# A two-layer hybrid decoder step on one core: output projection joined to the feed-forward network's first half, second half with six and three token tiles per unit of weights, RWKV output beside sample attention

## The reference, cut to what matters

```python
mix = jnp.concatenate([a_out, b_out], axis=-1)      # layer 1: [c_out (RWKV), d_out (sparse attention)]
x = x + mix @ w_out                                 # output projection, 1024 x 1024
...
def conv_ffn(x, g, w_in, conv_w, w_out, buf):       # x = x + conv_ffn(...)
    h = rmsnorm(x, g) @ w_in                        # 1024 -> 2 * 2816
    padded = jnp.concatenate([buf, h], axis=1)
    c = sum(padded[:, i:i + t_len] * conv_w[i] for i in range(3))
    gate, val = jnp.split(c, 2, axis=-1)
    return (jax.nn.silu(gate) * val) @ w_out, padded[:, t_len:]
...
# end of rwkv7_mixer: group norm per head, scale, bonus, gate
y = ((y - mean) * lax.rsqrt(var + RWKV_GN_EPS)).reshape(...) * ln_g + ln_b
out = (y + bonus) * g
```

## Time and profile before

| | us |
|---|---|
| median of 3 runs | 5395.19 (5392.64 to 5398.42) |
| profiled execution | 5434.91 |
| its span, first to last instruction | 5433.3 |
| PE busy | 4338.8 (80%) |
| DVE, ACT, POOL busy | 2336.0 (43%), 1099.4 (20%), 981.7 (18%) |
| mean granted TensorE clock | 0.815 of full speed |

### The profile page before, as it was taken

The page is one execution under the profiler, slowest core; times in us unless marked ns, Lnnn a source line. Parts: engine busy times, 40 slices in busy tenths (PEclk is TensorE's granted clock), DMA queues, the critical chain, the costliest instruction groups (busy, mean ns, idle before and its releaser), DMA issues. The chain is left out here.

```text
span 5433.3 us, 56566 instructions
## 1 busy us (share of the span) xinstructions
PE 4338.8 (80%) x21681; PEld 3367.2 (62%) x21681; DVE 2336.0 (43%) x3548; ACT 1099.4 (20%) x2122; POOL 981.7 (18%) x569
## 2 busy tenths in 40 slices
PE   7799958777899979799748657785276876999799
PEld 6566734335899956577613256775154355999667
DVE  3066431212556521210057567776694134556410
ACT  1132210110111122111034411211253101111221
POOL 2000000000222223222033265000001111222133
PEclk9955556888899989899755567877588987999899
DMA  3211010543111122222233220001313532111120
GB/s 128 79 23 24 12 28 16 161 143 109 48 46 46 35 69 67 85 93 76 83 109 122 99 73 15 28 28 32 109 39 106 159 114 77 46 46 46 61 69 30
DMA packets 239772, 377.90 MB, mean 70 GB/s; under 512 B 107035, under 2 KB 113964, under 8 KB 238191
## 3 DMA queue, kind: packets, MB, share of 16 engines
q1 hardware_dynamic: 213574, 285.77, 17.1%
q0 software_dynamic: 26000, 89.51, 5.3%
HBM read 292.93 MB, written 88.98 MB: 70 GB/s over the span
## 5 line engine op out<-in xcount | busy, mean ns | idle before, releaser
L91 PE MATMUL ffn_up_hp<-ffn_up_xT,ffn_up_w_high 128*128 128x352 f32 x4224 | 1016.1, 324 | 9.5 <-DVE ffn_up_xT L198 9.5
L91 PEld LDWEIGHTS ffn_up_hp<-ffn_up_xT,ffn_up_w_high 128*128 128x128 f32 x4224 | 736.7, 189 | 11.4 <-DVE ffn_up_xT L198 11.4
L91 PE MATMUL ffn_up_hp<-ffn_up_xT,ffn_up_w_low 128*128 128x352 f32 x2112 | 680.2, 322 | 0.0
L91 PEld LDWEIGHTS ffn_up_hp<-ffn_up_xT,ffn_up_w_low 128*128 128x128 f32 x2112 | 399.3, 189 | 0.0
L91 PE MATMUL ffn_down_acc<-ffn_down_w_high,ffn_down_a_high 128*128 128x512 f32 (+1 forms) x792 | 324.1, 409 | 81.4 <-DVE ffn_down_w_low L752 53.3
L91 PE MATMUL od_in_acc<-od_in_w_high,od_in_xT 128*128 128x512 f32 (+3 forms) x1152 | 353.6, 388 | 1.0 <-POOL od_in_w_low L273 1.0
L474 POOL TENSOR_TENSOR ffn_up_w_low<-ffn_up_w,ffn_up_w_high 128x1024 fp32r<-128x1024 f32 x88 | 211.3, 2401 | 756.9 <-DVE ffn_up_w_high L84 756.9
L91 PE MATMUL ffn_down_acc<-ffn_down_w_low,ffn_down_a_high 128*128 128x512 f32 (+1 forms) x792 | 319.4, 403 | 0.0
L91 PE MATMUL ffn_down_acc<-ffn_down_w_high,ffn_down_a_low 128*128 128x512 f32 (+1 forms) x792 | 318.0, 402 | 0.0
L728 POOL TENSOR_TENSOR ffn_down_a_low<-ffn_act_actT,ffn_down_a_high 128x768 fp32r<-128x768 f32 (+2 forms) x144 | 213.2, 1481 | 501.9 <-ACT ffn_down_a_high L700 501.9
L551 ACT ACTIVATE ffn_up_hb<-ffn_up_hp 128x352 f32<-128x352 f32 (+1 forms) x264 | 101.1, 456 | 882.8 <-PE ffn_up_hp L91 882.8
(11 more groups left out here) (573 smaller groups left out, 7993.5 us busy)
## 6 DMA issues: line engine op xcount, KB each, us to landing
ffn_up_w<-ffn_w_in POOLq DMA_DIRECT2D x88, 512.0 KB, 4.8
ffn_down_raw<-ffn_w_out SPq DMA_DIRECT2D x44, 512.0 KB, 3.9
sbs_pages<-cache_sb_k SPq DMA_DIRECT2D x64, 256.0 KB, 2.9
sbs_pages<-cache_sb_v SPq DMA_DIRECT2D x64, 256.0 KB, 3.0
rwkv_arrays<-rwi_out SPq DMA_DIRECT2D x8, 2048.0 KB, 12.3
dsas_pages<-cache_dsa_k SPq DMA_DIRECT2D x64, 256.0 KB, 3.0
dsas_pages<-cache_dsa_v SPq DMA_DIRECT2D x64, 256.0 KB, 3.0
od_in_w<-od_w_in POOLq DMA_DIRECT2D x7, 2048.0 KB, 10.9
```

What stands on the lines that cost most here:

```text
L91: last = nc.tensor.matmul(out, a[p], b[q], start=start and i == 0, stop=stop and i == 2)
```

## The change

Three things change. (1) `project(ev_out)` and `conv_ffn` become one block, `mix_and_ffn`, and od_out likewise: the whole w_mix is loaded in four pieces, all nine tiles are mixed with both column chunks, and each mixed tile is normed and turned from SBUF between the products of the next one. (2) In the second half of the FFN the loops become c, {tiles 0 to 5, tiles 6 to 8}, u, t, with eight accumulators. (3) `rwkv_output` loses its stage; its generators are woven with those of layer 1's sample attention, behind prompt attention. In both sample attentions the query copies take both rounds at once (32 copies for 64), and PE waits for the query and key rows alone.

```diff
-def conv_ffn(nc, name, src, gain, w_in, conv_w, w_out, state, dst, tails, ident_src):
+def mix_and_ffn(nc, name, mix, w_mix, resid, src, gain, w_in, conv_w, w_out, state, dst, tails, ident_src):
...
 @block.gpsimd
 def _(pool):
+    for p in range(PIECES):                                   # PIECES = 4, KP = 2
+        k = slice(p * KP, (p + 1) * KP)
+        pool.dma_start(raw_w[:, k, :], w_mix.rearrange("(k p) n -> p k n", p=P)[:, k, :]).then_inc(o_ld[p], 16)
     for q in range(2):
         load(pool, 0, q)
...
 @block.sync
 def _(sp):
-    s_start(sp)
+    sp.dma_start(ident[:, :], ident_src).then_inc(const_ld, 16)
+    for t in range(2):
+        sp.dma_start(mixed[0:rows_of(t), t, :], mix(t)).then_inc(mix_ld[t], 16)
     sp.dma_start(rows[0:2 * DEC_BATCH, :], state).then_inc(rows_ld, 16)
     sp.dma_start(rows[2 * DEC_BATCH:NR, :], conv_w).then_inc(rows_ld, 16)
-    t_sync(sp)
+    sp.dma_start(gain_b, gain.broadcast_to([P, D_MODEL])).then_inc(const_ld, 16)
+    sp.wait_ge(cols_tr, 1)
+    for t in range(NX1):                                      # NX1 = 3
+        sp.dma_start(x1[0:rows_of(t), t, :], resid(t)).then_inc(res_ld[t], 16)
+    for t in range(TT):
+        if t + 2 < TT:
+            sp.wait_ge(tr_ready, 2 * turn_of["mix", t] + 2)
+            sp.dma_start(mixed[0:rows_of(t + 2), t % 2, :], mix(t + 2)).then_inc(mix_ld[t % 2], 16)
+        sp.wait_ge(x1_ready, 2 * t + 2)
+        sp.dma_start(src(t), x1[0:rows_of(t), t % NX1, :]).then_inc(x1_st[t % NX1], 16)
...
 @block.tensor
 def _(pe):
+    pe.wait_ge(const_ld, 32)
+    turn_tile(pe, "mix", 0)
+    turn_tile(pe, "mix", 1)
     pe.wait_ge(rows_ld, 32)
-    pe.wait_ge(const_ld, 32)
     # 44 transposes of the state and tap rows, wait for DVE's copies of them
+    mixing(pe, 0, range(2))                                   # 48 products
+    for t in range(1, TT):
+        mixing(pe, t, [0])                                    # 24 products
+        if t + 1 < TT:
+            turn_tile(pe, "mix", t + 1)
+        mixing(pe, t, [1])
+        turn_tile(pe, "x1", t - 1)
     up(pe, 0, first=True)                                     # x1 tile 8 is turned before its third block
...
 @block.vector
 def _(dve):
+    turned_parts(dve, "mix", 0)
+    turned_parts(dve, "mix", 1)
     # four copies of the turned state and tap rows
+    for p in range(PIECES):
+        dve.wait_ge(o_high_done, p + 1)                       # ACT makes the high parts
+        nc.vector.tensor_tensor(o_low[:, k, :], raw_w[:, k, :], o_high[:, k, :], ALU.subtract).then_inc(o_low_done, 1)
+    mixed_row(dve, 0)
...
+    for t in range(1, TT):
+        if t + 1 < TT:
+            turned_parts(dve, "mix", t + 1)
+        turned_parts(dve, "x1", t - 1)
+        mixed_row(dve, t)          # 2 adds, wait for ACT's root, reciprocal, scaling
...
-        NB = 3
+        NB = 8
+        TOGETHER = [range(0, 6), range(6, TT)]
...
+order = [(c * TT + t, u) for c in range(NCH) for ts in TOGETHER for u in range(NU) for t in ts]
+place = {unit: m for m, unit in enumerate(order)}
+split_after = {max(first_use(0, u) - 4, 1): (0, u) for u in range(NU)}
+split_after.update({last_use(c - 1, u) + 2: (c, u) for c in range(1, NCH) for u in range(NU)})
...
+for m, (n, u) in enumerate(order):                            # ACT
+    at_least(act, unit_mm, m - 1)
+    nc.scalar.activation(unit_part(a_high, n, u), act_unit(n, u), ACT.Copy).then_inc(a_high_done, 1)
+    if m in split_after:
+        split_pieces(*split_after[m])
...
-        rwkv_output(nc, A, rw, ry, mix[1][:, 0:HALF])
-        attention_alone(nc, "dsa", A6, qn[prompt, :], kp, ...)
-        sample_attention(nc, "dsas", A6, qn[sample, :], ks, ...)
+        attention_alone(nc, "dsa", prompt_attention, A6, qn[prompt, :], kp, ...)
+        output_and_attention(nc, A6, rw, ry, mix[1][:, 0:HALF], qn[sample, :], ks, ...)
...
+def rwkv_output(nc, ph, A, rw, y_in, mix, pace=1.55):
+    step = lambda t, part: 0.6 + pace * (t + part)            # in units of attention items
+    # SP: first loads at 0, tile t >= 2 at step(t - 2, 1.0), after the store of tile t - 2
+    # DVE: parts at step(t, 0), (t, 0.4), (t, 0.8); ACT: Square (t, 0.2), Sqrt (t, 0.6); POOL: store (t, 0.9)
...
+            weave(a_sync(sp), o_sync(sp))                     # and so for every engine
```

More of the change, by code:

```diff
@@ L423, in conv_ffn @@
     EV = 4
+    NX1 = 3
+    PIECES = 4
+    KP = KT // PIECES
+    GAIN = 2 * KT * D_MODEL + (NX1 + 3) * D_MODEL
+    with Phase(nc, name + "_mix") as early:
+        o_high = early.sb("high", [P, KT, D_MODEL], F32R)
+        o_low = early.sb("low", [P, KT, D_MODEL], F32R)
     with Phase(nc, name + "_act") as outer:
@@ L613, in _ @@
                 combine(dve, 0)
+                for s in range(NX1):
+                    dve.wait_ge(x1_st[s], 16 * TT // NX1)
                 with dve.Fori(1, FT - 1) as j:
@@ new lines, in sample_attention @@
+    ident = ph.sb("ident", [P, P])
+    table = ph.sb("table", [1, DEC_BATCH * N_PAGES], I32)
+    pages = ph.sb("pages", [P, SLOTS, N_PAGES, HALF])
+    qk_rows = ph.sb("qk_rows", [NS, 2, HALF])
+    v_new = ph.sb("v_new", [DEC_SEQ, DEC_BATCH, HALF])
+    qkT = ph.sb("qkT", [P, 2, HP, NS])
+    Q = ph.sb("Q", [P, DEC_BATCH, HP, P])
+    kT = ph.sb("kT", [P, 2, HP, PAST_LEN])
+    ex = ph.sb("ex", [P, ALL])
+    cp = ph.sb("cp", [P, ALL + 1])
+    w = ph.sb("w", [P, ALL])
+    wT = ph.sb("wT", [P, N_PAGES + 1, P])
@@ new lines, in sample_attention @@
+    own_head = ph.sb("own_head", [R, HEADS])
+    late = ph.sb("late", [P, DEC_SEQ])
+    zero = ph.sb("zero", [P, 1])
+    tmp = ph.sb("tmp", [R, HALF])
+    out = ph.sb("out", [R, DEC_BATCH, HEAD_DIM])
+    if softmax:
+        sel = ph.sb("sel", [P, ALL])
+        near = ph.sb("near", [P, 256 + DEC_SEQ])
+        stat = ph.sb("stat", [P, 4])
+    ps_t = ph.ps("ps_t", [P, 2, NC_COLS])
+    ps_s = ph.ps("ps_s", [P, 3, NC_COLS])
+    ps_o = ph.ps("ps_o", [P, 2, NC_COLS])
+    table_ld = ph.sem("table_ld")
@@ new lines, in sample_attention @@
+    qk_ld = ph.sem("qk_ld")
+    ld = ph.sem("ld")
+    sel_ld = ph.sem("sel_ld")
+    page_ld = [ph.sem(f"page_ld{i}") for i in range(SLOTS)]
+    set_up = ph.sem("set_up")
+    qk_tr = ph.sem("qk_tr")
+    q_ready = ph.sem("q_ready")
+    unit_tr = ph.sem("unit_tr")
+    unit_ev = ph.sem("unit_ev")
+    s_mm = ph.sem("s_mm")
+    keep_done = ph.sem("keep_done")
+    own = ph.sem("own")
+    w_done = ph.sem("w_done")
+    pv_mm = ph.sem("pv_mm")
+    o_ev = ph.sem("o_ev")
+    out_ready = ph.sem("out_ready")
@@ L2064, in _ @@
[L2064 to L2075 removed]
+                    src = A["sel_sample"][b * DEC_SEQ:(b + 1) * DEC_SEQ, :]
@@ new lines, in tensor @@
+                    pe.wait_ge(unit_ev, u - 1)
+                    for i in range(4 if j < 2 else 1):
+                        src = w[:, (4 * j + i) * P:(4 * j + i + 1) * P] if j < 2 else w[:, PAST_LEN:ALL]
+                        last = nc.tensor.transpose(ps_t[0:src.shape[1], u % 2, i * P:(i + 1) * P], src, ident[:, :])
+                    last.then_inc(unit_tr, 1)
+                pe.wait_ge(unit_ev, (r + 1) * RU)
+            if b == 0:
+                pe.wait_ge(ld, n_ld)
+            at_least(pe, o_ev, b - 1)
@@ L3366, in _ @@
-            for s in range(2):
-                pool.wait_ge(st[s], 16 * ((TT + 1 - s) // 2))
+            weave(a_gpsimd(pool), o_gpsimd(pool))
+        @block.tensor
+        def _(pe):
+            weave(a_tensor(pe))
         @block.scalar
         def _(act):
-            act.wait_ge(set_up, 1)
-            for t in range(TT):
-                r, s = rows_of(t), t % 2
-                act.wait_ge(centred, t + 1)
-                nc.scalar.activation(sq[0:r, s, :], y[0:r, s, :], ACT.Square).then_inc(squared, 1)
-                act.wait_ge(var, t + 1)
-                nc.scalar.activation(stat[0:r, 2, :], stat[0:r, 1, :], ACT.Sqrt, bias=eps[0:r, :],
-                                     scale=1.0 / HEAD_DIM).then_inc(root, 1)
+            weave(a_scalar(act), o_scalar(act))
```

874 lines of the change are left out of this document (449 added, 425 removed).

## The result

After the change the kernel takes 5161.4 us (median of 4 runs, 5146.6 to 5166.1) where it took 5396.8 beside it (4 runs, 5392.6 to 5432.6): a ratio of 0.9545, 95% interval 0.950 to 0.959. The forecast was 5123, in a range of 5080 to 5195. The median fell by 235 us of the 272 forecast.

The account below looks back on a forecast made before the run. PE, busy four fifths of the span, was taken as the bound, with its waits at stage start-ups to be gained: 144 + 56 + 68 + 4 = 272 us off the 5395 median gives 5123, range 5080 to 5195.

Parts of the forecast that it names:

- Joined projection: Projection joined to the FFN's first half: pass 0 ends 169.5 us after stage start, not 241.7; 72 us gained, 144 in both layers.
- Rival 2: The joined loop goes by its hand-offs, not PE: eight tiles lose 8 x 7.8 us a layer, total 5248; chance 0.09.
- Second half: FFN's second half, six and three tiles for a unit of weights: 302 us for 329.7, 28 gained, 56 in both layers.
- the 12 us for splits: FFN's second half: 1.5 to 2 us lost for each of five splits, 4 where the units have four k-tiles.
- The 4 us for slow first products: FFN's second half: 4 us of the forecast 302 allowed for slow first products.
- Start and end: FFN's second half: 6.5 us of waiting for low weights stay at the start, and 4 us at the end.
- Rival 3: FFN's second half: PE waits for activation parts at each of 2 x 72 units, losing 350 us, total 5473; chance 0.03.
- RWKV output: The output's 75.7 us stage goes, its work woven into layer 1's sample attention: loss 8 us, gain 68.
- rival 1: The woven attention stage gives nothing: page loads behind store waits stall PE 8 us every tile, total 5191; chance 0.12.
- Table loads: Woven attention stage: ACT's five table switches at 1.28 us each, one counted on the path; the skill page says about 2.7.
- The port rule beside rival 1: Woven attention stage: POOL's issues could stand behind DVE's two-input instructions, as both lock shared ports; no separate size given.
- Start of sample attention: Sample attention with 32 query copies for 64: layer 0 gains 4 us; layer 1's 4 are lost to the wait for Square.

## Why the prediction was right, and what in it was off

- **Joined projection: right.** In layer 1: start S+16.6 (forecast 15), first product S+30.0 (29), tile 0 S+42.5 (42), 12.90 us a tile (12.9), end of pass 0 S+170.2 (169.5), 71.5 us for 72. Layer 0 got 68.7: there the norm's gain lands 1.9 us later and tile 0 takes 0.8 longer, which is most of the 4 us that are missing in both layers together. That PE's first turn waits for the gain was right, and the separate semaphore showed it. Rival 2 is refuted: the loop has no wait.
- **Second half: mechanism right, two terms mis-sized.** 40 us for 56. Of the sum, 18 x 15.3 + 6.5 + 12 + 4 + 4, the 12 us for splits became 19.5 in layer 1 (the gaps of 20.8 less a product's 0.23 each): I took 1.5 to 2 us a split where the gaps measure 2.6 to 3.7, and 4 where it is 6.1, and left out the first unit's 2.1. ACT waits 4.4 us for the third piece's load and PE has less in hand than I gave it. The 4 us for slow first products became 9.4, as the products behind four of the five splits are slow, too, and not those of the start alone. What made up for 5.5 us of this was luck: a tile's 15.31 us in the old order hold 0.3 us beyond its 66 products at 0.227, which the new order hardly pays, so the products take 269.9 us and not 275.4. Start and end came as forecast (6.3 and 4.0). The later third piece, which removes ACT's wait, gave 18.9 and 18.5 us. Rival 3 is refuted: besides the start, the gaps stand at six of the 72 units, not at each.
- **RWKV output: right, with a loss undersized, 61.4 for 68.** The room was there, and PE waits for no page load beyond the first item's, so rival 1 is refuted. I forecast 8 us lost, with 4 more of the shorter start that the Square takes back; by the undone stage it was 17.1. The early wait was 8.0 for the 3 + 4 forecast. Two table loads, not one, lie on the path, and a Square ahead of item 8's copies makes one wait before the scores 3.1 us where it is 0.7 without. For the slower products behind these waits, 4 us, I had no term.
- **Table loads.** ACT loads a table five times in that stage, 1.28 us each, as forecast; each of the two loads for Exp lengthens PE's wait from 5.6 to 6.8 us. The Trainium skill, "ScalarE: Activation LUTs", section "What ACT_TABLE_LOAD costs", has about 2.7 us a change, load and drain. This trace agrees with the load and shows no drain: 1.2 us on the path, and the three loads that stand right behind ACT's own work start within 0.02 us of its end, and ACT's next instruction within 0.02 us of theirs.
- **The ports.** The port rule beside rival 1, that DVE and GpSimd lock a shared pair of ports (the Trainium skill, "SBUF — State Buffer", list of terms), had no effect to be seen. The nine stores that the prediction went by could not have shown one: none of them, before or after, runs beside an instruction of DVE with two inputs. The 32 selection loads of the second round can: six of the RWKV output's two-input instructions of 0.69 us now run on DVE beside them, where none did before, and they take 15.76 us, 15.84 before.
- **Start of sample attention: right.** 3.9 us in layer 0 for 4. The copies were not undone in a run, but the two traces of layer 0 show it: PE's wait of 11.4 us before its first page was for the query copies and is now 11.0 us for the pages. That page is turned 15.0 us into the stage, 18.9 before; the copies end at 10.3 and the first item's last page lands at 14.9. In layer 1 the shorter start is worth 2.9 us (222.3 to 219.4 with the output undone), for 4.
- **The sum.** The changed stages gave 244.8 of 272 us: 16 are missing in the second half, 7 in the attention stage, 4 in the joined stages. Between 244.8 and the medians' 235.4 lies the untouched stretch's scatter. Taking the 272 from the median and not from the profiled execution was right, though not for the reason given (that waits and start-ups don't shrink in proportion): the profile of before had some 40 us in that stretch that no change could take.

## What to carry to other kernels

When a stage waits on its own start, run it inside the stage before and let the order on the busiest engine keep one tile in hand: here that hid a wait of 3.9 us a tile, worth 5.8. Where a load sits in an engine's fixed order ahead of work that the bottleneck needs, ask when it lands, and move the use back (the third piece of weights) or the load forward (y, for the first Square): it was the same mistake twice, and both were repaired by order alone. A semaphore that several loads share is as late as the last of them.

## What the runs showed of the hardware

A short wait of PE can cost more than itself, and not by its length alone. In the second half of layer 1 after the change, these windows follow gaps of 3.7, 2.6, 6.1 and 3.7 us:

```profile
4861.30:4866.00 4.70, 4.64 (x13) 3.69 (x14) 0.00 (x0) 0.00 (x0) 1.66 (x2) 0.64 0.32 109
...
4967.30:4972.00 4.70, 4.62 (x14) 1.97 (x15) 0.00 (x0) 0.00 (x0) 1.70 (x2) 0.64 0.34 112
...
5000.80:5005.50 4.70, 4.65 (x11) 1.88 (x12) 0.28 (x1) 0.00 (x0) 1.64 (x1) 0.50 0.57 167
4891.00:4895.50 4.50, 4.43 (x19) 3.68 (x20) 0.00 (x0) 0.00 (x0) 1.68 (x2) 1.00 0.68 224
```

Of two gaps of 3.7 us one was followed by a clock of 0.64 and one by 1.00, and a gap of 2.6 us was followed by 0.64. And the untouched S5 and prompt attention of layer 0, with the same 2072 matmuls, took 702 us in the one profile of before and 651 to 675 in the eleven profiles of kernels with the change or parts of it: here the windows of three kernels, before, after, and with the RWKV output undone.

```profile
262.02:963.55 701.53, 585.30 (x2072) 382.51 (x2072) 309.95 (x538) 156.55 (x336) 7.12 (x8) 0.57 0.10 23
```

```profile
262.90:920.44 657.54, 534.33 (x2072) 345.83 (x2072) 309.30 (x538) 155.20 (x336) 7.10 (x8) 0.62 0.11 24
```

```profile
264.06:915.44 651.38, 530.35 (x2072) 342.84 (x2072) 309.18 (x538) 155.52 (x336) 7.11 (x8) 0.62 0.11 24
```

The busy time of DVE and ACT is the same in all three; PE's differs by 55 us with the granted clock. What sets the clock there was not tried and stays open. That it is what scatters this kernel's runs is likely, not shown (the profiled execution of before, with the 702 us, took 39.7 us more than the median). The scatter is why stages and not totals carried most of the verdicts here.
